# Two running sums of squares per norm, with their column sums in another PSUM bank, in an 18-stage transformer kernel

## What is computed

```
def rmsnorm(x, g):
    xf = x.astype(jnp.float32)
    y = xf * lax.rsqrt(jnp.mean(xf * xf, axis=-1, keepdims=True) + EPS)
    return (y * g.astype(jnp.float32)).astype(x.dtype)
```

## Time and profile before

| | |
|---|---|
| median of three runs | 1830.99 us (1830.60 to 1831.76) |
| the profiled execution's own time | 1834.0 us |
| its span | 1832.2 us |
| TensorE busy | 1781.4 us, 97% of the span |
| VectorE busy | 1192.1 us, 65% |
| ScalarE busy | 844.5 us, 46% |
| GpSimd busy | 826.5 us, 45% |
| DMA | 297.69 MB, 162 GB/s on average |
| mean granted TensorE clock | 0.988 |

### The profile page before, as it was taken

The page is one execution under the profiler, slowest core; times in us unless marked ns, Lnnn a source line. Parts: engine busy times, 40 slices in busy tenths (PEclk is TensorE's granted clock), DMA queues, the critical chain, the costliest instruction groups (busy, mean ns, idle before and its releaser), DMA issues.

```text
span 1832.2 us, 37956 instructions
## 1 busy us (share of the span) xinstructions
PE 1781.4 (97%) x14134; PEld 1714.4 (94%) x14134; DVE 1192.1 (65%) x2236; ACT 844.5 (46%) x1294; POOL 826.5 (45%) x337
## 2 busy tenths in 40 slices
PE   8999999999999999999998999999999999999997
PEld 8999987788899998977998999999999999999997
DVE  6775675575355657747574999999995555544444
ACT  5444532455564445685444555544433333334443
POOL 4666585742766665700006789300014444444442
PEclk9999999999999999999998999999999999999998
DMA  7655453622445553533554555433345555555553
GB/s 248 220 181 186 143 178 113 194 93 84 161 148 184 184 186 112 185 126 103 167 181 149 172 185 178 158 130 130 128 139 184 183 183 183 183 184 184 183 185 102
DMA packets 83908, 297.69 MB, mean 162 GB/s; under 512 B 10244, under 2 KB 12709, under 8 KB 83558
## 3 DMA queue, kind: packets, MB, share of 16 engines
q1 hardware_dynamic: 81664, 290.82, 48.3%
q10 hardware_dynamic: 2150, 5.57, 0.9%
HBM read 295.30 MB, written 1.05 MB: 162 GB/s over the span
## 4 chain that ended last, share of the span: by engine, by line
PE 63%; issue 15%; POOL 12%; DVE 6%; ACT 1%; DMA 1%; POOLq 0%; SPq 0%; DVEq 0%; ACTq 0%
PE ps L1749 18%; PE ps L1751 18%; PE ps L1750 18%; POOL ring_lo L512 12%; PE ps L2261 2%; PE ps L1962 2%; DMA ring<-in_stream 1%; DVE ring_lo L1097 1%; PE ps L1930 1%; PE ps L1809 1%; PE ps L1810 0%; DVE arena L1287 0%; PE ps L1972 0%; DVE small L1289 0%; DVE aux L1618 0%
## 5 line engine op out<-in xcount | busy, mean ns | idle before, releaser
L1751 PE MATMUL ps<-h_hi,ring_lo 128*128 128x256 f32 (+1 forms) x2432 | 684.9, 282 | 0.0
L512 POOL TENSOR_TENSOR ring_lo<-ring,peer_split 128x1024 fp32r<-128x1024 f32 x128 | 315.0, 2461 | 472.3 <-ACT peer_split L621 466.6
L1751 PEld LDWEIGHTS ps<-h_hi,ring_lo 128*128 128x128 f32 x2432 | 459.1, 189 | 0.0
L512 POOL TENSOR_TENSOR ring_lo<-ring,main_hi 128x1024 fp32r<-128x1024 f32 x113 | 285.3, 2525 | 207.7 <-ACT main_hi L621 200.5
L621 ACT ACTIVATE peer_split<-ring 128x1024 fp32r<-128x1024 f32 x256 | 270.1, 1055 | 217.1 <-PE ps L1751 217.1
L512 POOL TENSOR_TENSOR ring_lo<-ring,more_hi 128x1024 fp32r<-128x1024 f32 x87 | 225.1, 2587 | 301.1 <-ACT more_hi L621 296.7
L1749 PE MATMUL ps<-h_hi,peer_split 128*128 128x256 f32 x1024 | 292.0, 285 | 3.3 <-POOL ring_lo L512 1.9
L1749 PE MATMUL ps<-peer_split 128*128 128x256 f32 x1024 | 289.3, 283 | 0.1
L1751 PE MATMUL ps<-peer_split,ring_lo 128*128 128x256 f32 x1024 | 288.8, 282 | 0.0
L1750 PE MATMUL ps<-peer_split 128*128 128x256 f32 x1024 | 287.9, 281 | 0.0
L1750 PE MATMUL ps<-h_lo,peer_split 128*128 128x256 f32 x1024 | 287.4, 281 | 0.0
(11 more groups left out here) (380 smaller groups left out, 3744.7 us busy)
## 6 DMA issues: line engine op xcount, KB each, us to landing
ring<-in_stream SPq DMA_DIRECT2D x550, 512.0 KB, 3.4
arena<-in_decay ACTq DMA_DIRECT2D x1, 1536.0 KB, 8.4
x<-in_x SPq DMA_DIRECT2D x4, 256.0 KB, 5.4
arena<-in_keys ACTq DMA_DIRECT2D x1, 1024.0 KB, 5.6
out<-h SPq DMA_DIRECT2D x4, 256.0 KB, 2.3
aux<-in_dft ACTq DMA_DIRECT2D x1, 816.0 KB, 9.0
aux<-in_idft ACTq DMA_DIRECT2D x1, 768.0 KB, 6.9
arena<-in_mask ACTq DMA_DIRECT2D x1, 768.0 KB, 6.6
```

Of the source, the lines that this page charges most:

```text
L512: nc.gpsimd.tensor_tensor(ring_lo[:, c % NS, :], ring[:, c % NS, :], hi_part(c).bitcast(F32), ALU.subtract).then_inc(lo_pool, 1)
L1751: return M(out, w_lo, parts[0], start=False, stop=stop, skip_group_check=True)
```

## The change

Each norm keeps two running sums, one over tiles 0, 2, 4, 6 and one over tiles 1, 3, 5, 7. Squares 0 and 1 go straight to the two places (for norms 0, 1, 3, 5, 7 and 8 the two halves of bank 6), VectorE makes six adds in place of seven, and an add waits for the add two before it. TensorE sums both totals over the partitions and accumulates them, with eight instructions in place of four (twelve in place of six in norm 6), and these column sums stand at column 500 of bank 7. In `down_squares` the high part stands behind squares 6 and 7. In norms 7 and 8 the places of the adds between the updates of x are fitted to this.

```diff
-        def running(n, w):
+        def running(n, k, w):
 
-            return squares_at(n)[:, 0, 0:w] if n in (2, 4, 6) else ps[:, 6, 512 - L:512 - L + w]
+            return squares_at(n)[:, k % 2, 0:w] if n in (2, 4, 6) else ps[:, 6, k % 2 * T:k % 2 * T + w]
+
+        def column_sum(p, c):
+
+            return ps[0:p, 7, slice(SUMS_AT + c.start, SUMS_AT + c.stop)]
...
-                A(squares_at(n)[:, k, 0:w] if k else running(n, w), src, ACT.Square).then_inc(sq_ready, 1)
+                A(squares_at(n)[:, k, 0:w] if k > 1 else running(n, k, w), src, ACT.Square).then_inc(sq_ready, 1)
...
                     else:
-                        hi_to(base + 3 * FT + 3)
                         act_e.wait_ge(chunk_done, base + 3 * FT)
                     squared_in(n, 2 * b, acc(2 * b))
                     squared_in(n, 2 * b + 1, acc(2 * b + 1))
+                hi_to(base + 3 * FT + 3)
...
                 dve.wait_ge(sq_ready, KT * n + k + 1)
-                if k > 1:
-                    dve.wait_ge(sq_added, (KT - 1) * n + k - 1)
-                total = running(n, w)
-                V.tensor_tensor(total if k < KT - 1 else squares_at(n)[:, 0, 0:w], total, squares_at(n)[:, k, 0:w], ALU.add).then_inc(sq_added, 1)
+                if k > 3:
+                    dve.wait_ge(sq_added, (KT - 2) * n + k - 3)
+                total = running(n, k, w)
+                V.tensor_tensor(total if k < KT - 2 else squares_at(n)[:, k % 2, 0:w], total, squares_at(n)[:, k, 0:w], ALU.add).then_inc(sq_added, 1)
...
-                for k in range(1, KT):
+                for k in range(2, KT):
...
-                if n > 1:
+                if n > 2:
                     add_square(7, n - 1)
...
-                if n == 3:
-                    add_square(8, 1)
-                elif n == 5:
-                    for k in (2, 3, 4):
+                if n == 5:
+                    for k in (2, 3):
                         add_square(8, k)
-            for k in (5, 6, 7):
+            for k in (4, 5, 6, 7):
                 add_square(8, k)
...
-                pe.wait_ge(sq_added, (KT - 1) * (n + 1))
-                for t, (t0, tn) in enumerate(LT[0:2] if w == T else LT):
-
-                    ins = M(ps[0:tn, 6, t:t + 1], squares_at(n)[:, 0, t0:t0 + tn], ones[:, 0:1], start=(t == 0), stop=True, skip_group_check=True)
+                pe.wait_ge(sq_added, (KT - 2) * (n + 1))
+                for a in range(2):
+                    for t, (t0, tn) in enumerate(LT[0:2] if w == T else LT):
+                        ins = M(column_sum(tn, slice(t, t + 1)), squares_at(n)[:, a, t0:t0 + tn], ones[:, 0:1], start=(t == 0 and a == 0), stop=(a == 1), skip_group_check=True)
                 ins.then_inc(ssq_ready, 1)
```

More of the change, by code:

```diff
@@ L367, in build @@
         N_SMALL, N_CONST = 5, 3
+        SUMS_AT = 500
         def acc(n):
@@ L584, in root @@
                 for p, c in token_tiles(w):
-                    ins = A(root_t[0:p, c], ps[0:p, 6, c], ACT.Sqrt, scale=(4.0 if half else 1.0) / D, bias=(eps_half if half else eps_full)[0:p, :])
+                    ins = A(root_t[0:p, c], column_sum(p, c), ACT.Sqrt, scale=(4.0 if half else 1.0) / D, bias=(eps_half if half else eps_full)[0:p, :])
                 ins.then_inc(std_ready, 1)
```

## The result

The changed kernel took 1834.06 us (median of 12 runs, 1832.84 to 1838.18); the kernel before took 1830.8 us beside it (12 runs, 1827.92 to 1836.65). The ratio is 1.0021, 95% interval 1.0013 to 1.003. The forecast was 1831.8 us and no difference that can be measured, with a range up to 1833.4: the measured time lies 0.66 us above that range. The profiled execution took 1834.97 us (span 1833.2, mean granted clock 0.987) against 1834.0 (span 1832.2, clock 0.988) before, so it is 1.0 us longer, where the sum of the terms was 0.75.

A forecast was written before the change was run, and what follows sets the result against it. TensorE, busy 97% of the span, bounds the kernel, so only its waits at the norms can be won. Terms sum to +0.75 us: 1834.0 to 1834.8 profiled, 1831.8 on the median, own range 1830.6 to 1833.0, wider 1829.2 to 1833.4.

The forecast's parts named there:

- The chain of norm 1, and norm 5: Norms 1 and 5: add 7 about 1.0 us earlier, column sums 0.44 longer; net -0.60 and -0.57 us.
- rival (c): VectorE still starts adds 0.54 apart in norms 0, 1, 3, 5 and 8: +4.4 us, 1835.4 us; chance 0.06.
- Norm 8: At the end, bound by VectorE alone: add 7 comes 1.11 us earlier, half-clock column sums cost 0.84; net -0.27.
- Norm 0: Last add starts 0.62 us earlier, column sums cost 0.44 more; net -0.18.
- The column sums: Four more cost 0.44 us, 0.84 at half clock; in norms 2, 4 and 6 0.37, 0.37 and 0.56, together +1.30.
- Norms 3 and 7: Norm 3: add 7 at 514.85, -0.21 + 0.44 = +0.23 us; norm 7: chains gain nothing, half-clock sums cost +0.84.
- Rival (a): Clock stays high behind norm 1 after a shorter stall: at most 2.25 us saved, 1829.5 us; chance 0.13.
- Rival (b): One more half-clock stretch, in norm 7: +2.25, together +3.0 us, 1834.0 us; chance 0.09.
- Rival (d): Behind norm 0 VectorE gets past GpSimd: 2.2 us go, sum -1.5, 1829.5 us; chance 0.04.
- The sum: Terms of all nine norms: about 3.5 us of stall goes, 4.3 us of matmul come, +0.75 us.
- half a microsecond of scatter in the runs: Run scatter allowed in the forecast's own range, 1830.6 to 1833.0 us, beside the adds' pitch and norm 8's clock.
- the same difference on the median gives 1831.8: Profiled execution, forecast at 1834.8 us, stands 3.0 us above the runs' median; the same difference gives 1831.8.

## Why the prediction was right or wrong

**The chain of norm 1, and norm 5: right.** Idle time 1.4 was said, 1.36 and 1.35 were found; -0.60 and -0.57 were said, -0.62 and -0.59 found. The pitch of 0.33 taken from another operation is that of the adds. That rules rival (c) out. The two kernels with one part each showed beyond it that the move and the chains need each other.

**Norm 8: right.** The idle time fell by 1.11, as worked out, and the column sums at half clock cost 0.85.

**Norm 0: right, but not by the first trace.** The last add came 0.62 earlier against its square, as said. In the first pair of traces the root gained 0.03 in place of 0.18, in the second pair 0.17. The difference is where ScalarE's squares end against TensorE's matmuls, 0.56 us before the last one in the first trace of the kernel before and 0.43 in the second; one trace doesn't give a term of 0.2 us here.

**The column sums: right in the chains, small by a fifth in the openings.** Eight take 1.02 and 1.84, as said. Inside an opening four more cost 0.45 and six more 0.67, a pitch of 0.11, not the 0.09 of the prediction, which set a single one's shortest duration against the time of six and so mixed durations of different places. Taken over norms 2, 4 and 6 it is 1.57 in place of 1.30. The Trainium skill, TensorE: Matmul & The Clock Gate, section LDWEIGHTS, gives 128 columns / 1.2 = 107 ns for such a load, with no term for the clock. The trace agrees at full clock (0.11) and not at half (1.84 for eight), so the prediction was right to go by the rows.

**Norms 3 and 7.** Norm 7 came at +0.86 for +0.84. Its half clock isn't fixed, though: in seven of the fourteen traces its column sums ran at full clock. For norm 3 the two parts of the term were right, -0.21 for the chains (0.20 found) and +0.44 for the sums. "Add 7 can go at 514.85" failed by what it took for given, that ScalarE's queue keeps its times. It hangs on the landing of a chunk, whose wait varied from 0.74 to 2.71 us, and in the first trace the sums were at half clock too. Norm 3 cost 0.55 to 2.8 in place of 0.23. The wait was longer in all seven traces with doubled column sums than in the six with single ones, so a part of this probably belongs to the change. What makes the chunk late stays open.

**Rival (a), the clock behind norm 1: it happened in part.** The fourteen traces bear it out. In the six with TensorE idle for 2.42 or 2.43 us before the column sums of norm 1, the granted clock from 205 to 220 us was 0.77 five times and 0.89 once. In the eight with 1.35 to 2.14 us it was 0.89 four times and 1.00 four times. All three traces of the changed kernel take 13.0 us from the column sums of norm 1 to those of norm 2, with 0.44 of added sums inside, and the two of the kernel before 14.24 and 13.47. So it gave 0.9 to 1.6 us net of these sums, where the prediction had at most 2.25 and a chance of 0.13. It did not make the kernel faster: other costs that the sum lacks stand against it, the landing at norm 3 and, in the first trace, a lower clock around norms 3 and 5. Rival (b) didn't happen in norm 7, where the clock over 955 to 985 us is 0.83 in both kernels. The Trainium skill, the same page, section HAM oscillation, says that idle gaps between bursts bring the half rate back. Norm 1 agrees, over the fourteen traces. Norm 5, whose idle time fell as much, is mixed: the clock from 705 to 730 us was 0.93 in both traces before, and 0.86, 1.00 and 1.00 in the changed kernel.

**Rival (d)** didn't happen. Behind norm 0 VectorE's two tiny operations took 2.45 us beside GpSimd's 2.41, as in the earlier trace rows, both moved together as the prediction argued:

```profile
21.02 2.45 DVE L1132 TENSOR_TENSOR small<-cols 128x1 f32<-128x1 f32 x2
21.04 2.41 POOL L517 TENSOR_TENSOR ring_lo<-ring,main_hi 128x1024 fp32r<-128x1024 f32 x1 [2.92 <-ACT main_hi L626]
```

**The sum: right at equal clock, with some luck.** +0.75 was said and about +0.8 is found over all runs, with a standard error of 0.3. But the traces have more in it than the sum had, on both sides: 0.3 more in the openings, 0.3 to 0.8 more in norm 3 (the second and third trace), and 0.9 to 1.6 less behind norm 1. That they nearly cancel was no part of the forecast.

**The step that failed** is "half a microsecond of scatter in the runs", and with it the range. Single runs of the kernel before have a standard deviation of 2.4 us, and its medians in the five groups of runs were 1830.8, 1831.38, 1831.77, 1831.8 and 1832.76 us. By an estimate from the table, the comparison's +3.3 is made of some +0.8 for the terms, some +0.9 for a lower mean clock, and the rest, about 1.5, for the scatter of these two series, since 35 and 119 runs give +1.75 (+-0.4, one standard error). In that series the mean clock of the changed kernel was 0.9875, the lowest of its three (0.9888 and 0.9887). The median of three runs that all numbers were based on stood 0.8 us below the mean of 119.

**The second step that failed** is "the same difference on the median gives 1831.8": it takes the mean clock of both kernels as equal. The four kernels with doubled column sums, 73 runs, have a mean clock of 0.9882, and the kernel before 0.9892, which by the slope is 1 us. Why these kernels have it isn't shown: width was tried and is not it. The three kernels with single column sums, the high part moved and at most four norms with two chains lie on the other side, 0.9906 to 0.9910. Behind norm 1 the clock goes with TensorE's idle time, and there the changed kernel gains. At the other places, where it must lose more than that, no rule comes out of the traces, and no run tells one cause from another.

## What to carry to other kernels

Read in each place of a pipeline which wait ends last before a general change is put into all of them: here a faster chain was worth 0.6 us in two norms and 1.1 in one, while its price on the bound engine was paid in all nine; joining the chains on an engine with spare time, and only where the chain is late, turned about +0.1% into -0.11 to -0.14%. A shorter stall can also be worth more than its length, by the clock behind it (norm 1). Where two limits stand close behind each other, take both away or expect nothing. For differences of a microsecond, compare the stretches of the timeline and the runs at equal granted clock; a dozen runs of each kernel don't decide, and a range for them must hold the scatter of the runs.

## What was not expected of the hardware

The time of this kernel goes with the mean granted clock, 1.04 us for 0.001, and this mean moves from run to run of the same program: 70% of the variance of 107 runs goes with it (0.84 squared), in a kernel whose work never changes. The pitch of a weight load with a one-column matmul is 0.11 us at full clock, among themselves and in a packed stream alike, and 0.21 at half clock. The landing of one input chunk at the same place in the program varied by 2 us between executions, and TensorE's idle time followed it one for one, 0.86 to 0.88 us above ScalarE's wait with one chain and 0.66 or 0.67 with two. A wait of TensorE that was shorter by 0.3 to 1.1 us was followed by a higher clock in nearly all traces (norm 1).
